# Weight slots of the two ffn stages at twelve different SBUF residues modulo 512

## The reference, cut to what matters

```python
for l in range(DEPTH_2):
    ...
    mix = jnp.concatenate([y_a, y_b, y_c], axis=-1)
    h = h + mix @ w_out[l]                       # 1024 x 1024
    hn = rms_norm_2(h, ffn_norm[l])
    gu = hn @ w_gate_up[l]                       # 1024 x 5632
    h = h + (jax.nn.silu(gu[..., :D_FF]) * gu[..., D_FF:]) @ w_down[l]   # D_FF = 2816
return rms_norm_2(h, final_norm)
```

## The kernel before, in words

| tiles | used in | residue |
|---|---|---|
| f_raw, f_hi, f_lo (all slots, both layers) | ffn | 480 |
| h_b_hi, h_b_lo; fT_hi, fT_lo | ffn | 480 |
| b_hi, b_lo (stream of the first block) | attention, scan, merge | 416 |
| h_x_hi, h_x_lo; yT_hi, yT_lo | attention, scan; merge | 480 |
| attT_hi, attT_lo | attention | 320 |
| mergedT_hi, mergedT_lo | merge | 416 |
| m_hi, m_lo (stream of the second block's inputs) | inputs (with h_b) | 288 |

## Time and profile before

### The profile page before, as it was taken

One profiled execution on the slowest core, in us unless ns is written; L12 is line 12 of the kernel. 1 busy time (PEld: TensorE's weight loads), 2 busy tenths in 40 slices (PEclk: granted clock), 3 DMA queues, 4 the chain that ended last, 5 costly groups with the idle time before them and its releaser, 6 DMA issues. The chain is left out here.

```text
span 3459.3 us, 44411 instructions
## 1 busy us (share of the span) xinstructions
PE 3082.9 (89%) x17561; PEld 2180.5 (63%) x17561; DVE 1388.7 (40%) x2258; ACT 1116.3 (32%) x1938; POOL 251.2 (7%) x278
## 2 busy tenths in 40 slices
PE   7999999999697877878787698889999998889999
PEld 5777888878533333333332585868888775778887
DVE  6872566653430000000000467553332467543332
ACT  4672666762200000000000435432222335332222
POOL 0000232210000000000000000300000000300000
PEclk9999999999799999999999799989999998999999
DMA  6322222234699999999998520023333420023322
GB/s 135 88 78 76 75 69 66 73 97 129 252 381 428 427 428 427 428 427 427 428 427 350 150 69 13 6 92 98 97 96 100 94 56 1 19 91 98 98 98 92
DMA packets 361295, 612.37 MB, mean 177 GB/s; under 512 B 73952, under 2 KB 308224, under 8 KB 336384
## 3 DMA queue, kind: packets, MB, share of 16 engines
q1 hardware_dynamic: 351152, 598.72, 47.4%
q0 software_dynamic: 9216, 8.42, 0.7%
q10 hardware_dynamic: 720, 2.36, 0.2%
HBM read 605.23 MB, written 23.07 MB: 182 GB/s over the span
## 5 line engine op out<-in xcount | busy, mean ns | idle before, releaser
L239 ACT ACTIVATE f_hi<-f_raw 128x1024 fp32r<-128x1024 f32 x148 | 156.6, 1059 | 521.8 <-PE ff_bk L299 521.7
L1857 PE MATMUL ex_gp<-ex_W,ex_XT 128*64 128x512 f32 x1024 | 253.8, 652 | 68.4 <-DMA ex_W<-in_w_expert_gate_dram 67.0
L1857 PE MATMUL ex_up<-ex_W,ex_XT 128*64 128x512 f32 x1024 | 237.9, 618 | 65.8 <-DMA ex_W<-in_w_expert_up_dram 65.8
L297 PE MATMUL ff_bk<-h_b_hi,f_hi 128*128 128x512 f32 x704 | 276.6, 393 | 2.8 <-DVE h_b_lo L3828 2.8
L298 PE MATMUL ff_bk<-h_b_lo,f_hi 128*128 128x512 f32 x704 | 276.1, 392 | 0.0
L299 PE MATMUL ff_bk<-h_b_hi,f_lo 128*128 128x512 f32 x704 | 275.8, 392 | 0.0
L248 DVE TENSOR_TENSOR f_lo<-f_raw,f_hi 128x1024 fp32r<-128x1024 f32 x148 | 180.5, 1223 | 209.7 <-ACT f_hi L239 209.4
L1886 PE MATMUL ex_yp<-ex_W,ex_hT 128*64 128x512 f32 x1024 | 226.8, 594 | 39.4 <-DMA ex_W<-in_w_expert_down_dram 32.4
L1900 DVE TENSOR_TENSOR ex_hid<-ex_sg,ex_up 128x512 f32<-128x512 f32 x32 | 22.0, 688 | 580.1 <-PE ex_up L1857 580.1
L1857 PEld LDWEIGHTS ex_gp<-ex_W,ex_XT 128*64 128x64 f32 x1024 | 91.7, 149 | 229.4 <-issue 227.6
L1857 PEld LDWEIGHTS ex_up<-ex_W,ex_XT 128*64 128x64 f32 x1024 | 86.4, 142 | 216.6 <-issue 216.6
(11 more groups left out here) (612 smaller groups left out, 6313.3 us busy)
## 6 DMA issues: line engine op xcount, KB each, us to landing
ex_W<-in_w_expert_up_dram SPq DMA_DIRECT2D x64, 2048.0 KB, 39.0
ex_W<-in_w_expert_down_dram SPq DMA_DIRECT2D x64, 2048.0 KB, 38.6
ex_W<-in_w_expert_gate_dram SPq DMA_DIRECT2D x64, 2048.0 KB, 39.0
b_raw<-in_w_in_dram SPq DMA_DIRECT2D x88, 512.0 KB, 3.9
f_raw<-in_w_gate_up_dram SPq DMA_DIRECT2D x88, 512.0 KB, 3.9
f_raw<-in_w_down_dram SPq DMA_DIRECT2D x44, 512.0 KB, 3.6
m_raw<-in_w_in_dram SPq DMA_DIRECT2D x20, 512.0 KB, 4.1
m_early<-in_w_in_dram SPq DMA_DIRECT2D x20, 512.0 KB, 4.1
```

The lines of the kernel that those rows point to most:

```text
L239: a.activation(self.hi[n % self.SLOTS][:, at], self.raw[n % self.RAW][:, at], ACT.Copy).then_inc(self.cast, 1)
L297: pe.matmul(out, a[0], b[0], start=first, stop=False)
L1857: ins = pe.matmul(ps[part[e], :], XT[b][:, q, part[e]], row_view(slots[e], KD)[:, q, :], start=(q == 0), stop=(q == KD - 1))
```

## The change

`Stream` gets an argument `apart`. Where it is given, one room of 6 · 4096 + 512 bytes is taken in place of the six hi and lo slots, and the slots are put into it by hand: slot i of hi at 4096 · i + apart[i], slot i of lo at 4096 · (3 + i) + apart[3 + i]. Only the two ffn streams give it. The raw slots stay. What is allocated after the room (fT and the small tiles of the stage) moves up by 512 bytes, which leaves its residue modulo 512 at 480.

The room begins at residue 480, so the number in `APART` is at the same time the distance modulo 512 from h_b and fT to the slot:

| | hi 0 | hi 1 | hi 2 | lo 0 | lo 1 | lo 2 |
|---|---|---|---|---|---|---|
| layer 0 | 32 | 64 | 128 | 256 | 384 | 448 |
| layer 1 | 96 | 160 | 192 | 224 | 320 | 352 |

No instruction is added, removed or moved on any engine, and every wait is the same; only addresses differ.

```diff
-    def __init__(self, k, ctx, tag, tiles, early=None):
-        self.tiles, self.issued, self.tag, self.early = tiles, 0, tag, early
+    def __init__(self, k, ctx, tag, tiles, early=None, apart=None):
+        self.tiles, self.issued, self.tag, self.early, self.apart = tiles, 0, tag, early, apart
...
-        self.hi = [k.sb(f"{self.tag}_hi{i}", [P, 1024], F32R, ctx) for i in range(self.SLOTS)]
-        self.lo = [k.sb(f"{self.tag}_lo{i}", [P, 1024], F32R, ctx) for i in range(self.SLOTS)]
+        if self.apart is None:
+            self.hi = [k.sb(f"{self.tag}_hi{i}", [P, 1024], F32R, ctx) for i in range(self.SLOTS)]
+            self.lo = [k.sb(f"{self.tag}_lo{i}", [P, 1024], F32R, ctx) for i in range(self.SLOTS)]
+        else:
+            room = k.sb(f"{self.tag}_room", [P, (6 * 4096 + 512) // 4], F32, ctx)
+            at = k.next_left() - (6 * 4096 + 512)
+            self.hi = [k.over(f"{self.tag}_hi_{'abc'[i]}", [P, 1024], F32R, at + 4096 * i + self.apart[i]) for i in range(self.SLOTS)]
+            self.lo = [k.over(f"{self.tag}_lo_{'abc'[i]}", [P, 1024], F32R, at + 4096 * (3 + i) + self.apart[3 + i]) for i in range(self.SLOTS)]
...
-        W = Stream(k, c0, f"f{l}", ffn_tiles(g("w_out"), g("w_gate_up"), g("w_down")))
+        W = Stream(k, c0, f"f{l}", ffn_tiles(g("w_out"), g("w_gate_up"), g("w_down")), apart=APART[l])
...
+APART = ((32, 64, 128, 256, 384, 448), (96, 160, 192, 224, 320, 352))
```

## The result

| | before | changed |
|---|---|---|
| median, us | 3456.91 (3 runs) | 3472.07 (3 runs, 3468.24 to 3474.41) |
| profiled execution, own time / span, us | 3461.08 / 3459.3 | 3472.07 / 3470.3 |

The ratio is 1.0048, 95% interval 1.0034 to 1.0062: slower by 15.2 us where 19.9 were forecast.

A forecast was written before the change was run, and what follows sets the result against it. PE's back-to-back matmuls were taken to bound the ffn stages; layer 0's +7.5 us and layer 1's +12.4 us gave +19.9 us, forecasting a median of 3476.8 us (+0.58%), range 3456 to 3488.

The forecast's parts named there:

- What bounds it: Both ffn stages: PE busy throughout, matmul after matmul 226.6 ns apart, so any added nanosecond reaches the program's end in full.
- distance 0 is the cheapest: Among the four distances the trace shows, 0 costs least, 226.7 ns from start to start; the others cost 2 to 8 more.
- The prices: Extra per ffn matmul: layer 0 4.2 ns, 7.5 us in all; layer 1 7.0 ns, 12.4 us.
- d and 512 - d are one: Assumption that a distance and its complement to 512 cost the same, taken from products of 256 columns at 64 and 192.
- For 32 I take the middle of 0 and 64, 1.1 ns: Layer 0, hi slot 0: unpriced distance 32 was given 1.1 ns per matmul.
- 64 costs 2.2 ns: From the merge stage's yT with b, 228.9 ns: 2.2 ns extra, used for 64 and 448 in layer 0.
- 224 and 256 lie nearest to 192: 6.6: Lo slots, 256 in layer 0 and 224 in layer 1: unpriced, each given 6.6 ns per matmul.
- 192 in layer 1's hi slot: Layer 1, hi slot 2: given 6.6 ns per matmul from the inputs' h_b with m, 233.3 ns.
- if layer 0 loses as much as layer 1: Sign that would refute the forecast: then not the distance is paid for, only being different from 0.
- Rival 2: Faster: equal residues collide, and some unpriced distances in ffn avoid the 13.3 ns; result 3439.0 us, chance 0.06.
- The 13.3 ns grow with the columns streamed: Argument that the excess over 213.3 ns is a cost of the stream itself, since 256 columns take 113 ns less.
- Rival 3: Slower in ffn: far distances cost more than 192, or changing distance between matmuls costs by itself; up to 3492 us, chance 0.12.

The follow-up runs named there:

- hi_or_lo: Changed kernel with a room 512 bytes wider: layer 0 hi slots at distance 0, lo at 64; layer 1 hi at 64, lo at 0; 3479.66 us.
- tile_mix2: Changed kernel with a wider room: hi and lo of a tile alike, tiles at 32, 64, 128 in layer 0 and 96, 160, 192 in layer 1; 3483.22 us.
- one64_96: Changed kernel with all six slots of layer 0 at distance 64 and all six of layer 1 at 96; 3480.16 us.
- one32_128: Changed kernel with all six slots of layer 0 at distance 32 and all six of layer 1 at 128; 3475.51 us.

## Why the prediction was right, point by point

**What bounds it.** Right. PE stayed busy for the whole of the long products and its waits stayed the same, so the extra time per matmul arrives in the stage's length, but for the clock of the first matmuls. ACT and DVE took 1060 and 1222 ns per tile (1059 and 1223 before).

**That distance 0 is the cheapest, so that leaving it costs time.** Right, and the experiments put it on firmer ground than four rows did: of the signed distances tried in ffn only 256 and +16 equal it, none beats it. In ffn only one operand of each pair was moved, so gate and up alone could be read as the price of the slot's own residue. The merge rows speak against that: a stationary operand at 416 goes at 228.9 ns with a moving one at 480, and at 227.0 with one at 416.

**The prices.** Here the working failed, in three terms that cancelled in part. Two assumptions were wrong: that d and 512 - d are one, and that the period is 512. The first was drawn from rows of 256 columns at distances 64 and 192, an order that holds for 256 columns only. What stands is a table of signed distances modulo 256, at 512 columns and full clock, of kernels whose slots all have one distance. It is taken from the starts of the single matmuls in the traces, to 0.1 ns, where the counts above are good to 0.2 ns or 1 ns; two numbers are two levels that the same distance took in different products:

| distance mod 256 | 0 | 8 | 16 | 32 | 64 | 96 | 128 | 160 | 192 | 224 | 240 | 248 |
|---|---|---|---|---|---|---|---|---|---|---|---|---|
| ns | 226.7 | 230.7 | 226.7 | 233.3 | 233.3 | 234.3 | 232.4; 233.3 | 233.3 | 228.9; 233.3 | 233.3 | 231.7 | 232.8 |

- "For 32 I take the middle of 0 and 64, 1.1 ns": it costs 6.6. The step "64 costs 2.2 ns" held for -64 alone; +64 costs 6.6. These two made layer 0 too cheap: 7.5 us forecast, about 8.9 us in the trace.
- "224 and 256 lie nearest to 192: 6.6": 256 is free.
- 192 in layer 1's hi slot was priced 6.6, after the inputs, where the distance is -192. At +192 it costs 2.2. This made layer 1 too dear: 12.4 us forecast, about 9.5 in the trace.

With the table's prices weighted over the slots, some 20 us come out, against 18.4 in the trace. The size was as good with the wrong prices as with the right ones, and that was luck: the forecast's sum was a mean over many distances, most of which cost 6 to 7 ns, and its errors had both signs. The prediction named this outcome as one that would refute it in part ("if layer 0 loses as much as layer 1"), and both layers do lose the same 5.3 ns in gate and up. The conclusion that it tied to this, that only being different from 0 is paid for, does not follow: the kernels with one distance per layer show 226.7, 228.9 and 233.3 ns. That the layers lose alike is a coincidence of their two sets of distances.

**The rule that the two reads do not disturb each other** (the Trainium skill: TensorE: Matmul & The Clock Gate, Part 2, "Step-by-step: what each phase is for"). By it no address would have a price. The runs disagree: in one kernel, slots at 256 give 226.7 ns in one layer and slots at 224 give 233.3 in the other, with the same instructions. That the moved operand's address acts through the weight load beside it is still an inference: the pairs that were varied are always stream and load, and exchanging them reverses the sign. No kernel without weight loads was run.

**Rival 2.** Its argument against was wrong although its verdict was right. "The 13.3 ns grow with the columns streamed" rested on 256 columns at distances other than 0. At distance 0 a matmul of 256 columns takes 120.0 ns, 106.7 + 13.3: the same 13.3 as with 512. So it goes with the matmul, or the load beside it, and at 256 columns other distances do save part of it (114 to 118 ns). At 512 none of the others did.

**Rival 3** asked whether a change of distance from matmul to matmul costs by itself. Inside a group of three it does in `hi_or_lo`, 2.1 ns in gate and up of both layers and some 5 ns in down; between tiles it does not (`tile_mix2`). In the changed kernel, where hi and lo differ too, it is not seen: the plain prices give 231.8 and 232.6 ns in gate and up, and 232.0 and 231.9 were measured.

**What stays open.** Down of layer 0 at APART 64 is at distance 192 and went at 233.3 ns, where four other readings of 192 (merge, +192, 448, and 320 exchanged) show 228.9; `tile_mix2` has 229.4 for it. The trace of `one64_96` has both levels in one stage, with the same slots and the same distance. The durations of out (first two rows) are those of merge, the durations of down (last row) are not:

```profile
L303 PE MATMUL ff_bk<-f_hi_b,fT_hi x14: 394/394/395, 2289.1 to 2307.7; 128*128 128x512 f32 x14
L304 PE MATMUL ff_bk<-f_lo_b,fT_hi x14: 388/388/389, 2289.4 to 2307.9; 128*128 128x512 f32 x14
...
L303 PE MATMUL ff_bk<-f_hi_b,fT_hi x30: 397/397/398, 2605.6 to 2659.5; 128*128 128x512 f32 x30
```

From start to start out goes at 228.9 ns and down at 233.3. At 2681 us, 16 us before the stage ends, down falls to 229 ns from one group of three matmuls to the next, without a pause of PE and with the same slots and distance. Exchanged 128 (layer 1 of `one32_128`) does the same on a smaller scale: 232.3 in out, 233.3 in down, some 232 from 3460 us on. So at these two distances the distance does not fix the pitch alone. That a state carried from one matmul to the next chooses between the levels would fit; no run shows it, and what makes them change was not found. Why +16 is free and -16 is not, and what the period of 256 comes from, was not tested either.

## What to carry to other kernels

When a stage is bound by matmuls back to back, let the moving and the stationary operand of the 512-column products begin at the same address modulo 256 bytes, and check it in the allocation: a few bytes of padding were worth 0.2% here, and scattering the buffers cost 0.5%. Measure the product's own shape, since with 256 columns the order was reversed. And when a price table is read off other stages, keep sign and period open: at 512 columns the rows of the kernel before had no distance with both signs, and one kernel with one distance per layer was enough to show that the sign counts.

## What the runs showed of the hardware that was not expected

- The pitch of a matmul with 512 columns at full clock depends on where its operands begin: 226.7 to 234.3 ns, with a period of 256 bytes (0 and 256, 192 and 448, 64 and 320 are alike) and with a sign (+64 233.3, -64 228.9).
- The same distance can show two levels in one execution: -64 went at 228.9 ns in out and 233.3 in down of layer 0 in `one64_96`, and at 229 again in its last 16 us.
- At distance 0 the pitch is 226.7 ns with 512 columns (512 / 2.4 GHz + 13.3 ns) and 120.0 ns with 256 (256 / 2.4 GHz + 13.3 ns). The Trainium skill (the same page, Part 1, "Wait — 56ns, not 53.3ns?") has 2.5 ns; no float32r stream with 512 columns and a stationary operand of 128 by 128 came near it, 226.7 ns being the least. At the half clock the 13.3 ns are absent.
- Steps as small as 8 bytes matter: 230.7 at +8, 226.7 at +16, 231.7 at -16.
